# Second block's input projections as three rounded passes, their weights loaded and split by half blocks

## The chip, the cores and the metric

One core of one Trainium2 chip runs the whole program. The metric is device microseconds (us) of one execution; lower is better. PE is TensorE, DVE VectorE, ACT ScalarE, POOL GpSimd, and SP the engine whose queue issues nearly all DMAs.

## The reference, cut to what matters

Two blocks follow each other. The first (two layers of gated attention, pooling and an MLP) gives `x`, 256 tokens of 1024. The second takes `x` and a context of 256 tokens:

```python
hl = rms_norm(xl, norm1_gain[layer]) * (1.0 + sc1l) + sh1l        # 256 latent tokens
hc = rms_norm(xc, norm1_gain[layer]) * (1.0 + sc1c) + sh1c        # 256 context tokens
pl = hl @ w_in[layer]
pc = hc @ w_in[layer]
al, bl, cl = jnp.split(pl, [A_PROJ, A_PROJ + B_PROJ], axis=-1)
...
a_lat, a_ctx = hgrn2_mixer(...)              # columns a: aq, ff, fb, ai, ag
b_lat, b_ctx = rwkv7_mixer(...)              # columns b
c_lat, c_ctxo = neighbourhood_attention(...) # columns cq, ck, cv
xl = xl + g1l * (jnp.concatenate([a_lat, b_lat, c_lat], axis=-1) @ w_out[layer])
... xl = xl + g2l * hierarchical_moe(h2l)    # 32 experts
```

All is float32. `w_in_2` is 1024 x 3968; the change is about `hl @ w_in` and `hc @ w_in`.

## The kernel before

Five instruction streams are written by hand and meet at semaphores. The first block splits each float32 operand in two rounded halves (type fp32r): `high` is a rounded copy made on ACT, `low` is what is left, made on DVE. A product is then three passes, high*high, low*high and high*low, summed in PSUM (`split_rows`, and L1345 for `down`). Weights go by half blocks of 8 x 256 columns: one ACT copy (L1840, L1842), one DVE subtraction (L2268, L2271), which writes `low` over the raw weights in the ring `wring` (`w_low` is the same memory). The second block does its projections in plain float32 instead: `project` (L1398, L1405) multiplies the raw blocks in `wring` with `hT` (8 tiles of 128 channels x 512 tokens). A plain float32 matmul leaves two records in the trace, a rounded pass one.

The order of the second block is the list `MIXER_STEPS`, which PE, ACT and DVE all walk: the projections of a, cq; then `carry` and `diag`; then seven times (`level` n, one of ck0 to ck3, cv0 to cv2); `cross`, cv3, `hsum`, then b0 to b7 between `window`, `qsum`, `ksq`, `qnorm`, `rope`, `knorm`, `vtok`, `kunit`; then the chunked inverse of the b mixer (`group` steps, which end with the job GT 3). Each product is a job with one of eight PSUM banks; a bank is opened when the job that held it has been emptied (`EARLIER2`). ACT takes most projections out of PSUM (L2031, L2042, L2053); b jobs end on DVE (`shift`, L2544 and L2545). In each level DVE makes the factors of the next level (`level_f`, L2556 to L2567), then puts four masked products in place (L2733); POOL makes those of the other direction (L3062 to L3073).

The weights of the projections are nine blocks of up to 2 MB in two slots of `wring`, slots 0 and 1; a block is loaded when the last job of the block before it in its slot is done. Slots 2 and 3 hold work data by then. After GT 3 the two blocks of `w_out_2` are loaded, and behind them on the same queue the experts' weights, 96 blocks of 2 MB in twelve slots, each slot as it comes free.

At the very start PE spreads the gain row `norm1` over the partitions through PSUM (L1277), DVE multiplies it into `x` (L2326), and PE turns the result (L1199), before the first products (L1227).

Of the kernel before, what the change touches and what calls it, by code (L numbers as in the profile page):

```python
# [13 lines left out]
P = 128  # L14
# [179 lines left out]
for _name, _n in (("norm1_gain_2", 8), ("rwkv_mu_2", 9), ("rwkv_kk_scale_2", 2),  # L194
# [9 lines left out]
BLOCKS2 = [("w_in_2", c, n) for c, n in ((0, 512), (512, 512), (1024, 256), (2432, 512), (2944, 512), (3456, 512),  # L204
                                         (1280, 512), (1792, 512), (2304, 128))]
N_BASE_DMA, N_EARLY_DMA, N_MOD_DMA = 13, 3, 4
EXPERT_ORDER = (4, 2, 3, 5, 6, 7, 8, 0, 9, 1, 10, 11)
BLOCKS2 += [("w_out_2", 512 * j, 512) for j in range(2)]
SLOT2 = [0, 1, 0, 1, 0, 1, 0, 1, 0] + [0, 1]
TURN2 = [SLOT2[:n + 1].count(SLOT2[n]) for n in range(len(BLOCKS2))]  # L210
B_WOUT = 9


BEFORE2 = [("ff", 1), ("ai", 1), ("ag", 0), ("cq", 1), ("ck", 3), ("cv", 3), ("b", 2), ("GT", 3), ("GT", 3)]


PROJ_C = {("aq", 0): (0, (0, P), S), ("ff", 0): (0, (2 * P,), 2 * S), ("ff", 1): (0, (3 * P,), 2 * S),
          ("fb", 0): (1, (0,), 2 * S), ("fb", 1): (1, (P,), 2 * S),
          ("cq", 0): (3, (0, P), S), ("cq", 1): (3, (2 * P, 3 * P), S),
          ("b", 0): (6, (0, P), S), ("b", 1): (6, (2 * P,), 2 * S), ("b", 2): (6, (3 * P,), 2 * S),  # L220
          ("b", 3): (7, (0,), 2 * S), ("b", 4): (7, (P,), 2 * S), ("b", 5): (7, (2 * P,), 2 * S),
          ("b", 6): (7, (3 * P,), 2 * S), ("b", 7): (8, (0,), S)}
PROJ_C.update({("ck", j): (4, (j * P,), 2 * S) for j in range(4)})
PROJ_T = {("ai", j): (1, (2 * j, 2 * j + 1), 2 * P, 4 * P) for j in range(2)}
PROJ_T.update({("ag", 0): (2, (0, 1), 0, 2 * P)})
PROJ_T.update({("cv", j): (5, (j,), 0, 4 * P) for j in range(4)})
# [26 lines left out]
def mixer_steps():  # L253


    steps = [("proj", job) for job in (("aq", 0), ("ff", 0), ("ff", 1), ("fb", 0), ("fb", 1), ("ai", 0), ("ai", 1), ("ag", 0),
# [3 lines left out]
    for n in range(len(LEVELS)):  # L260
# [5 lines left out]
              ("rope", 3), ("proj", ("b", 7)), ("kunit", 1), ("bstart", 0)]  # L266
    i = 0
# [34 lines left out]
def second_plan():  # L302
    both = ("act", "dve")
    jobs = [("vec", 0, "dve")]
    jobs += [("xc", j, both[j % 2]) for j in range(4)] + [("xl", j, both[j % 2]) for j in range(4)]
# [50 lines left out]
for _name, _j, _e in JOBS2:  # L356
    _count[_e] += 1
    EMPTIED2[(_name, _j)] = (_e, _count[_e])


def second_banks():


    order = [job[:2] for job in JOBS2 if job[0] != "wout"]
# [91 lines left out]
def build(nc, d, out):  # L456

    ctx = ExitStack()
    with ctx:
# [7 lines left out]
        def rounded_views(*pieces):  # L467


            with ExitStack() as over:  # L470
                return [over.enter_context(nc.sbuf_tensor(name, shape, F32R if name[:3] != "gap" else F32))
                        for name, shape in pieces]
# [18 lines left out]
                                           ("at_low", [P, HEADS_PER_GROUP, S]))  # L491
        R = sb("R", [P, R_SIZE])
# [43 lines left out]
        ones_row = R[0:1, 0:P]  # L536
        by_rms = R[:, P:P + ST * P].rearrange("p (t s) -> p t s", t=ST)
# [19 lines left out]
        first_in, ones_set, gain_full = sem("first_in"), sem("ones_set"), sem("gain_full")  # L557
# [103 lines left out]
        gmoe = part(D)  # L661
        mod2 = part(2, KT)
        mulT = part(3, KT)
        turn_area = at[0]
        base = part(P + 64 + 18 * 64)
# [4 lines left out]
        gmix = part(D)  # L670
# [13 lines left out]
        kam = part(2)  # L684
        route_area = at[0]
# [17 lines left out]
        fF, fB, kF, kB = part(2, T2), part(2, T2), part(2, T2), part(2, T2)  # L703
        ai, ag = part(4, A_W), part(2, A_W)
        hg_mask = part(len(LEVELS) * 2 * P // 4).bitcast(mybir.dt.uint8).rearrange("p (m t) -> p m t", t=P)
        junk2 = R[:, a_area:a_area + D]
        hT = part(KT, T2)
# [6 lines left out]


# [160 lines left out]
        def wait_block2(eng, n):  # L876

            eng.wait_ge(loaded[SLOT2[n]], 16 * (NB1 // SLOTS + TURN2[n]))

# [9 lines left out]
        def expert_loads(sw_, pair, m):  # L889

            each = 16 * 2 * TURN_BLOCKS // SLOTS_X
            i = expert_slot(m)
            earlier_loads = NB1 // SLOTS + SLOT2.count(i) if i < SLOTS else 0
            return sw_ * (TURNS // 2 * each) + pair * each + 16 * (earlier_loads + m // SLOTS_X + 1)
# [17 lines left out]
        def shift_parts(j):  # L912

            if j == 0:
                return [(pB_r[:, 0, :], 0, S, 0), (pB_r[:, 1, :], S, S, 1)]
            if j < 5:
                return [((pB_k, pB_v)[(j - 1) // 2][:, (j - 1) % 2, :], 0, T2, 1 + j)]
            return [((pB_w, pB_a, pB_g)[j - 5], 0, (T2, T2, S)[j - 5], 1 + j)]

# [4 lines left out]
        def _(sp):  # L924
# [47 lines left out]
            def early_load(j):  # L972
# [48 lines left out]
                elif j == 10:  # L1021
# [6 lines left out]
                    sp.wait_ge(sumsq2, 2)  # L1028
                    for i in range(2):
                        sp.dma_start((gmix, gmoe)[i].rearrange("p (q n) -> p q n", q=2),  # L1030
                                     mod_at(2 + 3 * i, 0, [[0, P], [SLOTS_E * 512, 2], [1, 512]])).then_inc(mod_in, 16)
# [4 lines left out]
            for t in range(ST):  # L1036
                sp.dma_start(h[:, t, :], d["x"][0, t * P:(t + 1) * P, :]).then_inc(h_in[t], 16)
            for n, (l, name, j) in enumerate(BLOCKS1):
# [51 lines left out]
            def load2(n):  # L1090
                name, c, width = BLOCKS2[n]
                dst = wring[:, SLOT2[n], 0:KT * width].rearrange("p (k n) -> p k n", k=KT)
                sp.dma_start(dst, d[name][0].rearrange("(k p) n -> p k n", p=P)[:, :, c:c + width])\
                    .then_inc(loaded[SLOT2[n]], 16)

            for n in range(len(BLOCKS2)):

                if n < 2:
                    wait_free(NB1 - SLOTS + n)
                else:  # L1100
                    wait_full2(sp, BEFORE2[n - 2])
                load2(n)
                if n == 1:
# [3 lines left out]
                if n == 2:  # L1107
                    sp.wait_ge(rpb_out, 16)
                    for q in range(2):
                        for r in range(6):  # L1110
                            src = bass.AP(tensor=rpb_dram.tensor, offset=(1 - q + r) * P,
                                          ap=[[1, 64], [7 * P, C_HEADS], [1, 64]])
                            sp.dma_start(nhank[64 * q:64 * q + 64, :, r, :], src).then_inc(nhank_in, 16)

# [32 lines left out]
        def _(pe):  # L1147
# [7 lines left out]
            def bias_table():  # L1155
# [10 lines left out]
                mm.then_inc(cols_full, 1)  # L1166

# [15 lines left out]
            for l in range(DEPTH):  # L1183
# [182 lines left out]
            def mix_out(j, ks, last):  # L1366

                half, t = j // 2, j % 2
                if not last:
                    wait_block2(pe, B_WOUT + half)  # L1370
# [5 lines left out]
                for k in ks:  # L1376
                    mm = pe.matmul(b[:, :], mixT[:, k, t * P:(t + 1) * P], w2(B_WOUT + half)[:, k, :],
# [6 lines left out]
            def w2(n):  # L1384
                width = BLOCKS2[n][2]
                return wring[:, SLOT2[n], 0:KT * width].rearrange("p (k n) -> p k n", k=KT)

            def project(name, j):

                in_channels = (name, j) in PROJ_C  # L1390
                n = (PROJ_C if in_channels else PROJ_T)[(name, j)][0]
                wait_block2(pe, n)
                b = fill(name, j)
                if in_channels:
                    _, tiles, width = PROJ_C[(name, j)]
                    for i, c in enumerate(tiles):
                        for k in range(KT):
                            mm = pe.matmul(b[:, i * width:(i + 1) * width], w2(n)[:, k, c:c + P], hT[:, k, 0:width],  # L1398
# [1700 lines left out]
```

## Time and profile before

| | |
|---|---|
| median of 3 runs | 1932.03 us (1921.66 to 1933.64) |
| profiled execution | 1936.39 us, span 1934.6 us |
| PE, DVE, ACT, POOL busy | 89%, 45%, 31%, 6% of the span |
| moved by DMA | 419.44 MB, mean 217 GB/s |

The span is the time from the first to the last record of one profiled execution. Busy shares are means over stages with different limits; the rows below are therefore read by stretches.

### The profile page before, as it was taken

Reading aid. Unit: us, or ns where it says so; the run is one execution under the profiler, and the core shown is the slowest. Engines: PE = TensorE matmul, PEld = TensorE weight load, DVE = VectorE, ACT = ScalarE, POOL = GpSimd, SP = SyncE. Lnnn points to the kernel's source line nnn. Section 1 sums busy time; section 2 is a strip of 40 time slices with the busy share of each in tenths; the row PEclk is TensorE's granted clock in tenths of the full one; section 3 lists DMA queues with packets and bytes.
Section 4 is the critical chain, followed back from the end, with each engine's and each line's share of the span. In section 5 each row is a group of like instructions: output and inputs, shape, how many; then the busy total and the mean of one; then the engine's idle time right before and its main releaser. Section 6 shows DMA issues by size and latency. Waiting matters only on the chain.

```text
span 1934.6 us, 32462 instructions
## 1 busy us (share of the span) xinstructions
PE 1729.6 (89%) x14383; PEld 1316.1 (68%) x14383; DVE 865.5 (45%) x1203; ACT 594.0 (31%) x768; POOL 114.8 (6%) x103
## 2 busy tenths in 40 slices
PE   7999999999999999999999999789987867767676
PEld 6999998997799999899857564578854222212221
DVE  4445556664444555666432745886524111101111
ACT  4435445443434544455321011333313000000000
POOL 0500000000050000000012420000000000000000
PEclk9999999999999999999999999899998887777877
DMA  7552365745775236596525110000089999999997
GB/s 278 212 199 77 131 234 219 277 176 182 256 256 200 75 131 234 219 331 216 177 50 141 59 44 11 2 3 3 4 316 396 409 410 409 409 410 410 409 410 290
DMA packets 154833, 419.44 MB, mean 217 GB/s; under 512 B 14051, under 2 KB 20894, under 8 KB 151636
## 3 DMA queue, kind: packets, MB, share of 16 engines
q1 hardware_dynamic: 154274, 417.35, 58.2%
q8 instruction: 103, 1.69, 0.4%
q10 hardware_dynamic: 434, 0.22, 0.0%
q14 instruction: 22, 0.18, 0.0%
HBM read 415.66 MB, written 1.89 MB: 216 GB/s over the span
## 4 chain that ended last, share of the span: by engine, by line
PE 63%; DMA 20%; DVE 9%; ACT 5%; issue 2%; SPq 1%; ACTq 0%; DVEq 0%
PE bank L1227 30%; DMA R<-w_exp_up 9%; DMA R<-w_exp_down 9%; PE ps_s L1345 3%; PE bank L1398 3%; PE ps_s L1398 3%; PE ps_t L1345 3%; ACT w_high L1842 2%; PE bank L1423 2%; PE bank L1796 2%; PE ps_t L1405 1%; DVE w_low L2271 1%; DMA wring<-w_up 1%; SPq L1126 1%; PE ps_t L1398 1%
## 5 line engine op out<-in xcount | busy, mean ns | idle before, releaser
L2271 DVE TENSOR_TENSOR w_low<-wring,w_high 128x2048 fp32r<-128x2048 f32 (+1 forms) x127 | 285.2, 2245 | 312.9 <-ACT w_high L1842 312.5
L1842 ACT ACTIVATE w_high<-wring 128x2048 fp32r<-128x2048 f32 (+1 forms) x127 | 236.2, 1860 | 341.1 <-PE bank L1227 297.4
L1227 PE MATMUL bank<-x_high,w_high 128*128 128x256 f32 x1600 | 326.2, 285 | 9.7 <-DVEq L2317 7.4
L1227 PE MATMUL bank<-x_low,w_high 128*128 128x256 f32 x1600 | 321.6, 283 | 0.0
L1227 PE MATMUL bank<-x_high,w_low 128*128 128x256 f32 x1600 | 320.3, 282 | 0.0
L1227 PEld LDWEIGHTS bank<-x_high,w_high 128*128 128x128 f32 x1600 | 248.2, 191 | 16.8 <-DVEq L2317 8.5
L1227 PEld LDWEIGHTS bank<-x_high,w_low 128*128 128x128 f32 x1600 | 248.1, 190 | 0.0
L1227 PEld LDWEIGHTS bank<-x_low,w_high 128*128 128x128 f32 x1600 | 247.1, 190 | 0.0
L1796 PE MATMUL bank<-R 128*32 128x512 f32 x640 | 96.5, 736 | 48.1 <-DMA R<-w_exp_up 37.8
L1796 PEld LDWEIGHTS bank<-R 128*32 128x32 f32 x640 | 19.6, 124 | 118.7 <-DMA R<-w_exp_up 65.0
L2986 DVE TENSOR_TENSOR R<-bank,R 128x512 f32<-128x512 f32 x8 | 5.5, 694 | 210.3 <-PE bank L1796 210.3
L2268 DVE TENSOR_TENSOR w_low<-wring,w_high 128x2048 fp32r<-128x2048 f32 x22 | 50.4, 2292 | 60.3 <-ACT w_high L1840 60.3
L1796 PE MATMUL bank<-wring,R 128*32 128x512 f32 x384 | 53.2, 677 | 22.4 <-DMA wring<-w_exp_up 22.4
L1227 PE MATMUL bank<-w_high,x_high 128*128 128x256 f32 x320 | 64.7, 284 | 5.0 <-issue 3.2
L1811 PE MATMUL ps_s<-R 128*32 128x512 f32 x192 | 32.8, 760 | 38.2 <-DMA R<-w_exp_down 32.7
L2994 DVE TENSOR_TENSOR R<-ps_s,R 128x512 f32<-128x512 f32 x8 | 5.5, 692 | 136.0 <-PE ps_t L1811 136.0
L1227 PE MATMUL bank<-w_high,x_low 128*128 128x256 f32 x320 | 64.4, 283 | 0.0
L1227 PE MATMUL bank<-w_low,x_high 128*128 128x256 f32 x320 | 63.9, 281 | 0.0
L1840 ACT ACTIVATE w_high<-wring 128x2048 fp32r<-128x2048 f32 x22 | 42.1, 1916 | 70.9 <-PE ps_t L1345 58.0
L2193 ACT ACTIVATE R<-bank,R 128x128 f32<-128x128 f32 x32 | 12.1, 456 | 168.6 <-PE bank L1778 168.6
L3026 POOL TENSOR_TENSOR R<-R 128x542 f32<-128x542 f32 (+3 forms) x20 | 33.0, 1650 | 497.7 <-ACT R L1871 496.3
L1398 PE MATMUL bank<-R,wring 128*128 128x256 f32 (+1 forms) x192 | 54.9, 445 | 2.6 <-DMA wring<-w_in 1.5
(617 smaller groups left out, 2731.9 us busy)
## 6 DMA issues: line engine op xcount, KB each, us to landing
wring<-w_in SPq DMA_DIRECT2D x36, 2048.0 KB, 8.2
R<-w_exp_up SPq DMA_DIRECT2D x24, 2048.0 KB, 24.0
R<-w_exp_down SPq DMA_DIRECT2D x24, 2048.0 KB, 23.8
wring<-w_up SPq DMA_DIRECT2D x22, 2048.0 KB, 9.2
R<-w_exp_gate SPq DMA_DIRECT2D x16, 2048.0 KB, 23.4
wring<-w_exp_gate SPq DMA_DIRECT2D x16, 2048.0 KB, 23.7
wring<-w_ada SPq DMA_DIRECT2D x12, 2048.0 KB, 10.3
wring<-w_down SPq DMA_DIRECT2D x10, 2048.0 KB, 7.7
```

The lines of the kernel that those rows point to most:

```text
L1126: sp.dma_start(expert_block(m).rearrange("p (u k n) -> p u k n", u=QUAD, k=k), src[:, :, k * c:k * c + k, :]).then_inc(loaded[s], 16)
L1227: mm = pe.matmul(b[:, i * S:(i + 1) * S], left, right, start=k == 0 and m == 0 and i == 0, stop=k == last and m == 2, skip_group_check=True)
L1345: mm = pe.matmul(down_bank[j], left, ww[:, kk, half * 512:(half + 1) * 512], start=i == 0 and kk == 0 and m == 0, stop=i == N_DOWN - 1 and ...
L1398: mm = pe.matmul(b[:, i * width:(i + 1) * width], w2(n)[:, k, c:c + P], hT[:, k, 0:width], start=k == 0, stop=k == KT - 1)
L1423: mm = pe.matmul(b[q, 64 * o:64 * o + 64], lhs(q, c), rhs(q, c), start=start, stop=stop, skip_group_check=skip)
L1796: mm = pe.matmul(banks8[2 + which][q, :], xg[:, k, q], ww[:, u, k % 2, :], start=k == 0, stop=k == KT - 1)
L1811: mm = pe.matmul(banks8[5 + half][q, :], hidT[:, k, q], ww[:, u, half * 512:(half + 1) * 512], start=k == 0, stop=k == D_EXP // P - 1)
L1840: a.activation(down_high(l, job[1]), down_rows(l, job[1], wring), ACT.Copy).then_inc(w_high_ready, 1)
L1842: a.activation(high_of(l, job), half_block(l, job, wring), ACT.Copy).then_inc(w_high_ready, 1)
L2268: v.tensor_tensor(down_rows(l, job[1], w_low), down_rows(l, job[1], wring), down_high(l, job[1]).bitcast(F32), ALU.subtract).then_inc(w_lo ...
L2271: v.tensor_tensor(half_block(l, job, w_low), half_block(l, job, wring), high_of(l, job).bitcast(F32), ALU.subtract).then_inc(w_low_ready, 1)
L3026: chain(g_eng.tensor_tensor(dst[:, :, 0:m], src[:, :, 0:m], src[:, :, w:w + m], ALU.add))
```

## The change

1. The inputs of the projections are split: `hT_high` on ACT, `hT_low` on DVE, tile pairs at a time, the 256 latent tokens before the 256 of the context. All their PSUM banks now count as emptied when DVE's `low` is written.
2. `project` makes three rounded passes.
3. `w_in_2` comes as 16 half blocks (`IN2`) in four half slots, in the memory of slots 0 and 1. Half block n is loaded when the last job of n - 4 is done. Its `high` is written to one of five areas of the second block's store that are free by then (`HOME2`), its `low` over the raw weights. The two steps of each split stand in the ACT and DVE streams as the steps `split` of `MIXER_STEPS`, behind the job that `SPLIT_BEHIND` names; block 0 is split in the last layer's `down`, blocks 1 and 2 between the two halves of the inputs.
4. The job ag comes after aq; DVE's first part of `carry` becomes a step `carry_in` behind fb1.
5. Loads of `gmix` and `gmoe` move behind b7, those of `nhank` from behind block 2 to behind half block 12.
6. At the start the gain row is loaded to all partitions by one DMA of 512 KB on SP's queue, ahead of the first weights; PE's spreading products are gone.
7. PE issues products whose result nobody reads (`keep_clock`): 6 at the start, 6 before the first `products` step, 5 before the router's counts, 2 before the experts, each a plain float32 matmul of 128 x 128 by 512 columns.

```diff
+IN2 = [(0, 256), (1024, 256), (256, 256), (512, 256), (768, 256), (2432, 256), (2688, 256), (2944, 256), (3200, 256),
+       (3456, 256), (3712, 256), (1280, 256), (1536, 256), (1792, 256), (2048, 256), (2304, 128)]
...
+HOME2 = "EXGECGECGECEFEFE"
+TAKEN_FROM = {2: None, 3: ("aq", 0), 4: ("xc", 3), 5: ("ff", 1), 6: ("fb", 1), 7: ("ai", 1), 8: ("cq", 0), 9: ("cq", 1),
+              10: ("ck", 1), 11: ("cv", 1), 12: ("ho", 1), 13: ("b", 0), 14: ("b", 2), 15: ("b", 4)}
+SPLIT_BEHIND = {("aq", 0): 3, ("ag", 0): 4, ("ff", 1): 5, ("fb", 1): 6, ("ai", 1): 7, ("cq", 0): 8, ("ck", 0): 9, ("ck", 1): 10,
+                ("cv", 1): 11, ("b", 0): 13, ("b", 2): 14, ("b", 4): 15}
...
+            if g == ("fb", 1):
+                with_splits.append(("carry_in", 0))
+        if step == "hsum":
+            with_splits.append(("split", 12))
...
+            for n, (c, width) in enumerate(IN2):
+                if n in (0, 2):
+                    wait_free(NB1 - SLOTS + n // 2)
+                elif n > 3:
+                    wait_full2(sp, LAST_JOB[n - 4])
+                if n == 5:
+                    sp.wait_ge(high2_ready, 3)
+                sp.dma_start(raw2(n, wring), w_in2[:, :, c:c + width]).then_inc(sem_of_in2(n), 16)
...
             def project(name, j):
...
+                pe.wait_ge(low2_ready, n + 1)
                 b = fill(name, j)
...
+                for k in range(KT):
+                    if k % 2 == 0 and job in (("aq", 0), ("ff", 0)):
+                        wait_emptied2(pe, ("xl" if name == "aq" else "xc", k // 2))
+                    for m, (wx, xx) in enumerate(((ww[0], hT_high), (ww[0], hT_low), (ww[1], hT_high))):
+                        for i, c in enumerate(tiles):
+                            left, right = (wx[:, k, c:c + P], xx[:, k, 0:width]) if in_channels else \
+                                (xx[:, k, c * P:(c + 1) * P], wx[:, k, :])
+                            mm = pe.matmul(b[:, i * width:(i + 1) * width], left, right, start=k == 0 and m == 0 and i == 0,
+                                           stop=k == KT - 1 and m == 2, skip_group_check=True)
...
+            def high_in2(n):
+
+                a.wait_ge(sem_of_in2(n), loads_of_in2(n))
+                if n >= 3:
+                    wait_full2(a, TAKEN_FROM[n])
+                a.activation(high2(n), raw2(n, wring), ACT.Copy).then_inc(high2_ready, 1)
...
+                    ins.then_inc(hT_act, 1)
+                    a.wait_ge(hT_act, (first + j) // 2 + 1)
+                    rounded(j)
+                    a.wait_ge(hT_dve, (first + j) // 2 + 1)
+                    rounded(j + 1)
...
+            high_in2(1)
+            x2_evac("xl", 0, 0)
+            high_in2(2)
+            x2_evac("xc", 1, 4)
...
+            def low_in2(n):
+
+                v.wait_ge(high2_ready, n + 1)
+                v.tensor_tensor(raw2(n, w_low), raw2(n, wring), high2(n).bitcast(F32), ALU.subtract).then_inc(low2_ready, 1)
...
+                for j in range(4):
+                    v.wait_ge(hT_ready, first + j + 1)
+                    v.tensor_tensor(hT_low[:, 2 * j:2 * j + 2, part_of], hT[:, 2 * j:2 * j + 2, part_of],
+                                    hT_high[:, 2 * j:2 * j + 2, part_of].bitcast(F32), ALU.subtract).then_inc(dve_emptied2, 1)
...
+            x2_evac("xl", 0, 0)
+            low_in2(1)
+            low_in2(2)
+            x2_evac("xc", 1, 4)
...
                 if l == 0:
-                    pe.wait_ge(ones_set, 1)
-                    pe.wait_ge(gain_in, 16)
-                    for half in range(2):
-                        mm = pe.matmul(ps_t[:, half * 512:(half + 1) * 512], ones_row, grow[0:1, half * 512:(half + 1) * 512],
-                                       start=True, stop=True)
-                    mm.then_inc(gain_full, 1)
+                    pe.wait_ge(idle_set, 1)
+                    keep_clock(bank[3][:, :], idle_in[:, 0:P], idle_in, 6)
...
                 elif stage == "products":
+                    if g == 0:
+                        keep_clock(open_bank("tk", 0)[:, :], ident[:, :], h[:, 0, 0:512], 6)
                     pe.wait_ge(group_ready, g + 1)
...
+            b = fill("tot", 0)
+            keep_clock(b[:, :], ident[:, :], h[:, 1, 512:1024], 5)
             pe.wait_ge(moe_c_in, 32)
             pe.wait_ge(sel_ready, 1)
...
+            keep_clock(banks8[3], ident[:, :], h[:, 1, 512:1024], 2)
             pe.wait_ge(rt_done, 1)
```

## Rows read from the trace of the kernel before

**Rows 1.** The page's first part: busy us, share of the span, instructions.

```profile
PE 1729.6 (89%) x14383; PEld 1316.1 (68%) x14383; DVE 865.5 (45%) x1203; ACT 594.0 (31%) x768; POOL 114.8 (6%) x103
```

**Rows 2.** Chain of waits over the span, second block: start, us, what.

```profile
985.65 22.87 PE bank L1398 x64
...
1036.12 8.28 DMA wring<-w_in
...
1065.64 7.08 PE ps_s L1398 x16
...
1133.27 7.06 PE ps_t L1405 x16
...
1190.71 8.94 PE ps_s L1398 x16
...
1242.29 4.51 PE bank L1423 x96
1246.80 1.87 PE ps_s L1423 x64
```

**Rows 3.** Windows: us; PE, PEld, DVE, ACT, POOL busy; PEclk, DMA share, GB/s.

```profile
985.65:1058.60 72.95, 71.50 (x258) 50.01 (x259) 8.50 (x15) 9.91 (x16) 15.29 (x12) 0.97 0.41 94
1058.60:1133.30 74.70, 74.40 (x393) 44.22 (x391) 57.16 (x80) 6.31 (x11) 34.23 (x48) 1.00 0.17 57
1133.30:1226.80 93.50, 90.95 (x340) 49.26 (x341) 48.84 (x72) 17.17 (x26) 1.71 (x1) 0.96 0.09 28
985.60:990.00 4.40, 4.35 (x11) 3.54 (x12) 2.93 (x6) 0.00 (x0) 0.00 (x0) 0.54 0.01 4
1234.00:1242.30 8.30, 0.01 (x2) 0.01 (x2) 7.96 (x13) 6.86 (x15) 0.00 (x0) 0.58 0.00 0
1430.00:1455.00 25.00, 23.51 (x332) 16.89 (x329) 9.38 (x23) 4.10 (x7) 0.00 (x0) 1.00 0.78 295
...
1476.60:1500.00 23.40, 21.70 (x174) 10.79 (x178) 3.76 (x14) 5.36 (x9) 0.00 (x0) 0.90 1.03 409
```

**Rows 4.** Chain of waits, first block: rounded passes that wait for nothing.

```profile
146.44 5.71 PE bank L1227 x48
...
467.66 2.80 PE ps_s L1345 x12
```

**Rows 5.** Timeline of ACT: a weight split, then projections taken out of PSUM.

```profile
965.38 1.92 ACT L1840 ACTIVATE w_high<-wring 128x2048 fp32r<-128x2048 f32 x1 [3.68 <-PE ps_t L1345]
...
994.80 0.60 ACT L2031 ACTIVATE R<-bank 128x512 f32<-128x512 f32 x1 [10.08 <-PE bank L1398]
...
1058.59 0.60 ACT L2031 ACTIVATE R<-bank 128x512 f32<-128x512 f32 x1 [6.32 <-PE bank L1398]
```

**Rows 6.** Timeline of DVE: a weight split, one level, the last steps ahead of the groups.

```profile
967.33 2.29 DVE L2268 TENSOR_TENSOR w_low<-wring,w_high 128x2048 fp32r<-128x2048 f32 x1 [3.31 <-ACT w_high L1840]
...
1096.60 1.31 DVE L2567 TENSOR_TENSOR R<-R 128x128 f32<-128x128 f32 x1
...
1098.43 0.45 DVE L2567 TENSOR_TENSOR R<-R 128x128 f32<-128x128 f32 x1
1098.92 2.56 DVE L2733 COPY_PREDICATED wring<-R,bank 128x512 f32<-128x512 uint8 x4
...
1213.04 0.75 DVE L2544 SCALAR_TENSOR_TENSOR R<-ps_s,R 128x510 f32<-128x510 f32 x1 [5.44 <-PE ps_s L1623]
...
1229.16 0.69 DVE L2790 TENSOR_TENSOR wring<-wring 128x512 f32<-128x512 f32 x1
```

**Rows 7.** DMA issues by shape: count, KB each, median us to landing.

```profile
wring<-w_in SPq DMA_DIRECT2D x3, 1024.0 KB, 7.2
```

**Rows 8.** Chain of waits, the start.

```profile
6.37 3.79 PE ps_t L1277 x4
10.24 2.48 DVE R L2326 x4
...
21.34 22.88 PE bank L1227 x192
```

More of the change, by code:

```diff
@@ L207 @@
+N_BASE_DMA, N_EARLY_DMA, N_MOD_DMA = 13, 3, 2
 EXPERT_ORDER = (4, 2, 3, 5, 6, 7, 8, 0, 9, 1, 10, 11)
[L208 to L222, printed above, removed]
@@ L266, in mixer_steps @@
               ("rope", 3), ("proj", ("b", 7)), ("kunit", 1), ("bstart", 0)]
+    with_splits = []
+    for step, g in steps:
+        with_splits.append((step, g))
+        if step == "proj" and g in SPLIT_BEHIND:
+            with_splits.append(("split", SPLIT_BEHIND[g]))
+            if g == ("fb", 1):
+                with_splits.append(("carry_in", 0))
+        if step == "hsum":
+            with_splits.append(("split", 12))
+    steps = with_splits
     i = 0
@@ L302, in second_plan @@
 def second_plan():
-    both = ("act", "dve")
     jobs = [("vec", 0, "dve")]
-    jobs += [("xc", j, both[j % 2]) for j in range(4)] + [("xl", j, both[j % 2]) for j in range(4)]
+    jobs += [("xc", j, "dve") for j in range(4)] + [("xl", j, "dve") for j in range(4)]
     for step, g in MIXER_STEPS:
@@ L660, in build @@
         at[0] = 0
-        gmoe = part(D)
         mod2 = part(2, KT)
         mulT = part(3, KT)
+        at[0] += -at[0] % 16
+        e_area = at[0]
+        gmoe = part(D)
         turn_area = at[0]
+        gmix = part(D)
         base = part(P + 64 + 18 * 64)
@@ L1113, in _ @@
                             sp.dma_start(nhank[64 * q:64 * q + 64, :, r, :], src).then_inc(nhank_in, 16)
+            wait_full2(sp, ("b", 7))
+            for i in range(2):
+                sp.dma_start((gmix, gmoe)[i].rearrange("p (q n) -> p q n", q=2),
+                             mod_at(2 + 3 * i, 0, [[0, P], [SLOTS_E * 512, 2], [1, 512]])).then_inc(gmul_in, 16)
+            wait_full2(sp, ("GT", 3))
+            for half in range(2):
+                name, c, width = BLOCKS2[half]
+                sp.dma_start(w2(half), d[name][0].rearrange("(k p) n -> p k n", p=P)[:, :, c:c + width]).then_inc(loaded[half], 16)
             gates_d = [d[x].rearrange("a g e k n -> (a g e) k n") for x in ("w_exp_gate_2", "w_exp_up_2", "w_exp_down_2")]
@@ L1166, in bias_table, with keep_clock @@
                 mm.then_inc(cols_full, 1)
+            def keep_clock(b, left, right, n):
+                for _ in range(n):
+                    pe.matmul(b, left, right, start=True, stop=True)
             def modulate(l, i):
@@ L1995, in _ @@
                 for i in range(2, N_DOWN):
+                    if l == DEPTH - 1 and i == N_DOWN - 1:
+                        high_in2(0)
                     a.wait_ge(down_used, l * (N_DOWN - 1) + i - 1)
@@ L2016, in full_bank, with x2_evac, rounded @@
                 return bank2(*job)
-            def x2_evac(name, dst, w, mul, add):
+            def x2_evac(name, c, first):
+                part_of = slice(0, S) if c == 0 else slice(S, T2)
+                def rounded(j):
+                    a.activation(hT_high[:, 2 * j:2 * j + 2, part_of], hT[:, 2 * j:2 * j + 2, part_of], ACT.Copy).then_inc(hT_ready, 1)
                 for j in (0, 2):
@@ L2116, in _ @@
                     project(*g)
+                elif step == "split":
+                    high_in2(g)
                 elif step == "carry":
@@ L2693, in _ @@
                     shift(g[1])
-                elif step == "carry":
+                elif step == "split":
+                    low_in2(g)
+                elif step == "carry_in":
                     v.wait_ge(base_in, 16 * N_BASE_DMA)
```

153 lines of the change are left out of this document (78 added, 75 removed).

## The prediction

> **What bounds the kernel now.** I read the page first: PE is busy for 89% of the span [rows 1], which says where to look but not what is worth what. Then the chain of waits, which names what ended last at each time. From 985.65 us, where the second block's projections begin, it is PE nearly throughout [rows 2]: the windows give 71.5, 74.4 and 91.0 us of PE in stretches of 73.0, 74.7 and 93.5 us, with DVE at 8.5, 57.2 and 48.8 [rows 3]. So up to about 1213 us each microsecond taken off a projection comes off the path, as long as DVE keeps up; the middle stretch is the one to watch. From 1213.04 to the end of L2790 at 1229.85 the chain is DVE's, fed by the job b5 [rows 6]. The groups follow and end with GT 3 at some 1412 us, and this job releases w_out and the experts' weights on SP's queue. From there to the last expert DMA is the limit: 409 GB/s and a share of 1.03 in 1476.6 to 1500, with short gaps before it (0.78 in 1430 to 1455) [rows 3]. The expert stretch has a fixed length from GT 3 on: what is saved before GT 3 shifts the end one for one, and a faster PE after it saves next to nothing.
>
> **The passes.** The unit here is one projection of 128 output columns by 512 tokens (or as much work): 8 plain matmuls of 512 columns, 16 records, 7.08 us as channels, 7.06 as tokens [rows 2]. After the change it is 24 rounded passes of 512 columns or 48 of 256. Twelve of the first kind take 2.80 us [rows 4], so 24 take 5.60; 48 of the second take 5.71 [rows 4]. Both rows are in the same number format with their weight loads hidden, so I take them as they are. There are 25.5 units: a and cq 10, ck and cv 8, b0 7.5. By stretches:
>
> - *aq.* Now it starts at 985.65 and ACT takes it at 994.80 [rows 5], 9.15 us, because the granted clock is 0.54 in 985.6 to 990, near the lower of its two levels, 1.2 GHz, after a pause of PE [rows 3]; that stretch gives about 2.2 us of work less than 2.4 GHz would. Afterwards aq waits tile pair by tile pair. The turned latent inputs arrive at 982.4 as now; ACT makes two 0.5 us evacuations and two rounded copies of 0.6 us per pair of jobs, DVE the same share plus 0.69 us for each `low` (my estimate from the 512-element rows of the same kinds of instruction). The first pair is split at about 985.1, the last at 987.7. With the same 2.2 us lost, 5.71 becomes 7.9: done at 993.0, a gain of **1.8**. Bounds: warm at once 3.9; nothing before the last pair, 0 or 1 lost.
> - *ag, ff, fb, ai, cq.* Now 63.8 us from 994.80 to 1058.59 [rows 5]. This holds a wait of 1.4 us at 1044.4 for the load that was issued at 1036.12 [rows 2]. Afterwards 4 x 5.60 + 5 x 5.71 = 51.0: gain **12.8**. The context tiles are split by 997, ff0 asks for them at 998.7. The wait goes, since half block n is asked for only three blocks after its load is issued: at least 20 us here against 7.2 to landing [rows 7] plus 4.2 for the split.
> - *Levels and cv3.* 1065.64 to 1133.27 is 67.6 us [rows 2] and holds seven projections, 49.6; afterwards 4 x 5.60 + 3 x 5.71 = 39.5. With 1.35 on cv3 the gain is 11.4, if DVE keeps up. DVE now has 57.2 us of work in 74.7 [rows 3]; splits 9, 10 and 11 add 3 x 2.29 [rows 6], 64.0 us in a stretch of 63.3. It is then full. What saves PE is that it asks only for the first two products of `level_f`, a projection later. I walked it through: a level step of DVE is 7.44 us (1094.04 to 1101.48; its last 2.56 us are the masked copies [rows 6]), a PE period 8.35. Split 9 also makes DVE wait for ACT (ck0 done, 0.6 evacuation, 1.92 copy [rows 5]). After splits 9 and 10 DVE is late by about one split, and the fourth product of level 3 finds its bank not emptied for 1.4 us. I take 1.5 off: gain **9.9**.
> - *b0 to b5.* These six take 43.8 us in the chain, one of them 8.94 at a lowered clock behind products of only 8 rows [rows 2]. Afterwards 5.71 + 4 x 5.60 + 7.8 for the slow one, 35.9: gain 7.9. Split 12 stands behind `hsum`, where ACT has 3.9 us of squares first; block 12 is ready as b1 wants it, within 0.2 us. Splits 12 and 13 make DVE late for `hout` and the first window products, so the last window waits some 1 us for a bank. Gain **6.9**.
> - *After b5* the DVE chain of 16.8 us [rows 6] stays as it is; split 15 lies before it. b6 and b7 lie beside it, worth nothing. Second block together: 1.8 + 12.8 + 9.9 + 6.9 = **31.4**.
>
> **Splits of the weights.** 16 x 1.92 us of ACT and 16 x 2.29 us of DVE [rows 5, 6]. In the stretches of rows 3 ACT has 9.9, 6.3 and 17.2 us of work, so ACT is nowhere near full; DVE hides all but the levels, as said. Behind a waiting `high_in2` on ACT are the evacuations of the next job; the loads are long in. Block 0 is split in `down`, where DVE idles 3.31 us before each split [rows 6]: 0. Queue SP: 16 issues in place of 9, the twelve of nhank moved behind half block 12, with b0's load (13) due only when cv1 is done: 0. gmix and gmoe behind b7 are wanted 200 us later: 0.
>
> **The start.** PE's spreading goes (6.37 to 10.16) and the DVE products can begin when the gain row is in. Rows of 512 KB from h land 1.3 us after each other, so I estimate 7.6 instead of 10.24 [rows 8]. The first turn would be ready at 11.3. But six idle products stand before it. At the rate of rows 8 (0.95 us a record, two records each) they take 11.4 us and end at 17.7; at full rate 5.3. Six products are dense work like aq's, so I take aq's loss, 2.2 us [rows 3]: 7.5 us, an end near 13.5, since the load of the identity is no longer second on its queue and lands some 0.5 us sooner, and then turns at full rate. DVE is then last: L1227 at 19.6 instead of 21.34, gain **1.7**. Bounds: 2.5 gained, 3.3 lost. The weights come 1.3 us later for the 512 KB, covered by 20 us.
>
> **The fills.** PE is idle in 1234 to 1242.3 at 0.58 of the clock, and the first 96 products then take 4.51 us where 64 take 1.87 later [rows 2, 3]; at that rate 2.8. Six fills of 5.3 us (7.5 with the 2.2 lost) end before 1242.3: gain **1.7**, bounds 2.5 gained and 2.4 lost if they run slow all along. The other seven are behind GT 3 under the DMA: 0, and 0 if slow, since at 1476 about three expert blocks of 5 us each are still to land before PE's first slot is wanted.
>
> **Sum.** 31.4 + 1.7 + 1.7 = 34.8. The profiled execution gives 1936.4 - 34.8 = 1901.6. It lies 4.4 above the median of the runs; from the median, 1932.0 - 34.8 = **1897**.
>
> **Rivals.** *A, DVE and POOL hold the levels.* L2567 takes 1.31 us with POOL at work and 0.45 after [rows 6]: the two slow each other. If each of splits 9, 10 and 11 keeps POOL's factors waiting for its 2.29 us and this passes to PE, 6.9 us go, and some 4 more where DVE is late for the windows: 1908. The Trainium skill, page "SBUF — State Buffer", section "Summary: rules for kernel authors", says a DVE instruction with two SBUF inputs and a GpSimd one that reads SBUF exclude each other for a whole instruction; the 1.31 agrees, and by it each split can hold POOL up for 2.29. Against A: POOL has 34.2 us of work in 74.7 [rows 3], and its factors are wanted one projection, 5.6 us, after they are begun. *B, slower: the splits are not hidden.* If blocks 1 to 15 were each split when PE already waits, 15 x (1.92 + 2.29) = 63 us come on the path: 1897 + 63 = 1960. It turns the sign when 2.3 us of each are exposed. Against it: all but split 12 stand two or more jobs before their use. *C, it gives more:* runs like the lowest of before (1921.7) on a shift of 36 give 1886. *D, the fills cost in both places* (3.3 and 2.4 lost in place of 1.7 and 1.7 gained): 9 us less, 1906.
>
> **How the numbers follow.** Forecast 0.60, A 0.16, D 0.09, C 0.08, B 0.03, and 0.04 for a gain under 1% by some stall that I don't see. The range must hold the forecast, A, C and D: 1885 to 1911. A change of under 1%, 19 us, can't be told from none here; the threshold is 1912.7, which A and D stay below: of these cases 0.93 lie below it, and I leave 0.03 of A's for a dearer stall: faster 0.90, same 0.07, slower 0.03.
>
> **What would show it.** Right: no L1398 or L1405 records of two per matmul; 24 passes in 5.6 us; no DMA wait ahead of cq; cq1 taken out at about 1042 (start shifts included), the chain at GT 3 near 1377; the first 96 group products in 2.8 us. A shows as PE waiting before `level` steps for POOL or DVE; B as PE waiting for DVE's `low` with ACT ahead of it; D as L1227 after 22 us. Wrong altogether if the rounded passes run slower with these operands than in the first block, or if the experts' stretch from GT 3 to the end, 522 us, changes.

## The result, and the profile after

The changed kernel takes **1904.3 us** (median of 4 runs, 1897.3 to 1906.0) against 1929.7 of before beside it (1921.7 to 1933.6): ratio 0.987, 95% interval 0.984 to 0.989. On two more chips it came to 0.985 [0.983, 0.986] and 0.983 [0.981, 0.986], 29.8 and 29.7 us less by the medians. So the change gives 25 to 30 us; 34.8 were forecast. The profiled execution took 1903.4, 33.0 less than that of before.

The page of after, its first part and the granted clock in 40 slices:

```profile
PE 1712.9 (90%) x14777; PEld 1347.8 (71%) x14777; DVE 907.9 (48%) x1227; ACT 627.0 (33%) x792; POOL 125.6 (7%) x103
...
PEclk9999999999999999999999999789999977767777
```

PE's share of the span hardly moves [rows 1], so this part says nothing of where 33 us went. In the clock's line a 7 and an 8 stand in slices 26 and 27 (1188.4 to 1283.5 us), where the groups begin. The chain of waits says more, piece by piece against rows 2 and 8: the start, the second block's first projection, the first level's projection, cv3, b4, and a piece of the groups.

```profile
5.29 7.88 PE bank L1222 x12
...
19.10 24.42 PE bank L1283 x192
...
981.55 18.68 PE bank L1451 x120
...
1046.88 5.78 PE ps_s L1451 x24
...
1107.67 5.91 PE ps_t L1451 x48
...
1159.59 7.82 PE ps_s L1451 x24
...
1183.13 3.36 DVE wring L2880
...
1258.51 2.85 PE bank L1469 x64
```

No DMA stands between 981.55 and cq: the load of 8.28 us at 1036.12 [rows 2] is gone from the chain. The last line is a product of 64 records that takes 1.87 us at the high clock [rows 2]. The same stretches in windows (columns as in rows 3): aq's beginning, all to the carry's products, the levels, the gates, the first expert loads, the end.

```profile
981.50:986.00 4.50, 4.45 (x27) 4.49 (x28) 4.23 (x5) 4.44 (x7) 0.00 (x0) 0.67 0.01 4
981.50:1045.00 63.50, 63.15 (x435) 58.47 (x436) 37.03 (x39) 29.48 (x36) 22.01 (x16) 0.97 0.39 117
1046.80:1107.60 60.80, 60.22 (x449) 53.09 (x448) 56.55 (x72) 10.02 (x11) 37.81 (x42) 1.00 0.31 79
1192.70:1203.40 10.70, 10.70 (x17) 4.34 (x17) 8.90 (x10) 5.77 (x8) 0.00 (x0) 0.50 0.29 58
...
1448.00:1471.00 23.00, 20.55 (x182) 8.95 (x186) 4.41 (x18) 5.66 (x9) 0.00 (x0) 1.00 1.02 409
1891.90:1901.50 9.60, 5.62 (x24) 1.85 (x24) 4.24 (x7) 0.00 (x0) 0.00 (x0) 0.99 0.30 109
```

PE is as full as before in the first two stretches, and they are shorter. DVE is busy for 56.6 of 60.8 us in the levels. The fourth line is the gates (products L1500 and L1502, 16 records, behind b7): they run at a granted clock of 0.50, which is 1.2 GHz, and over the 7.2 us of the gates before the clock was 0.76. The fifth is the expert loads' 409 GB/s, the same as before [rows 3].

The timeline of ACT answers to rows 5 (aq and cq1 taken out of PSUM), that of PE shows what became of the gates, of the fills behind them and of the first group products:

```profile
991.55 0.58 ACT L2096 ACTIVATE R<-bank 128x512 f32<-128x512 f32 x1
...
1039.83 0.60 ACT L2096 ACTIVATE R<-bank 128x512 f32<-128x512 f32 x1 [3.31 <-PE bank L1451]
```

```profile
1192.70 2.04 PE L1500 MATMUL bank<-R 64*128 64x512 f32 x2 [3.87 <-issue]
...
1203.37 7.87 PE L1222 MATMUL bank<-h,ident 128*128 128x512 f32 x12
1211.18 3.02 PE L1469 MATMUL bank<-ident,wring 64*64 64x64 f32 x96
```

Before, the gates ran from 1226.80 to 1233.97 behind a pause of PE of 2.56 us. Now the pause is 3.87 and they take 10.7. The fills then take 7.9 and end only as the products begin: DVE's input for these was ready at 1210.91, so the slow fills held them back by some 0.2 us.

From these points come the stretches of every kernel (us, the start of one piece less the start of another; L2880, L2789 in before, is the reciprocal behind b5; "last load" is where the last w_exp_down lands):

| kernel | first block's products | second block's | to L2880 | to group products | to w_out | to last load | to end |
|---|---|---|---|---|---|---|---|
| before | 21.3 | 985.7 | 231.0 | 25.6 | 170.2 | 508.2 | 14.0 |
| before, second profile | 21.3 | 982.3 | 230.7 | 25.6 | 170.5 | 508.2 | 12.5 |
| after | 19.1 | 981.6 | 201.6 | 28.0 | 172.5 | 508.2 | 9.6 |
| c0_after | 18.9 | 980.2 | 203.0 | 26.9 | 173.7 | 507.3 | 13.0 |
| c1_after | 19.3 | 982.3 | 201.6 | 26.8 | 172.9 | 508.6 | 9.7 |
| e1_no_fills | 19.1 | 979.2 | 201.6 | 26.8 | 171.2 | 506.7 | 11.1 |
| e2_gates_fill | 18.6 | 979.0 | 203.2 | 25.0 | 172.1 | 508.1 | 11.0 |
| e3_split10_later | 19.2 | 980.2 | 202.4 | 26.2 | 170.0 | 507.6 | 9.7 |
| e4_no_low_levels | 19.0 | 981.8 | 201.2 | 26.0 | 169.9 | 507.5 | 9.6 |
| e5_plain | 18.9 | 980.0 | 231.9 | 26.8 | 170.8 | 508.6 | 11.2 |
| e6_pauses_filled | 18.0 | 980.9 | 201.0 | 25.1 | 169.6 | 507.6 | 9.6 |
| e6b_pauses_filled | 18.7 | 979.8 | 201.9 | 25.0 | 170.2 | 507.2 | 11.1 |
| e7_start_as_before | 21.5 | 984.9 | 202.8 | 26.0 | 169.9 | 507.5 | 9.6 |
| e9_end_fills | 19.2 | 980.1 | 202.4 | 25.0 | 170.1 | 508.1 | 9.7 |

Between before and after: 29.4 us gained in the projections, 2.2 at the start and 1.9 more until 981.55; 2.4 lost ahead of the group products and 2.3 in the groups; 4.4 gained at the end, which is no part of the change, as c0_after shows with 13.0 for the same kernel.

### The profile page after: what moved, and what is told of

Read it like the earlier page. It is cut to its first block, busy times and chain, and to the rows that moved or that the text cites. A ratio compares the mean times of both kernels' runs of the same rounds, so it can differ in the third digit from the quotient of the medians.

```text
span 1901.5 us, 33316 instructions
## 1 busy us (share of the span) xinstructions
PE 1712.9 (90%) x14777; PEld 1347.8 (71%) x14777; DVE 907.9 (48%) x1227; ACT 627.0 (33%) x792; POOL 125.6 (7%) x103
## 4 chain that ended last, share of the span: by engine, by line
PE 62%; DMA 19%; DVE 10%; ACT 6%; issue 2%; DVEq 0%; ACTq 0%
PE bank L1283 30%; DMA R<-w_exp_up 9%; DMA R<-w_exp_down 9%; PE bank L1451 3%; PE ps_s L1397 3%; PE ps_t L1397 3%; ACT w_high L1889 2%; PE ps_s L1451 2%; PE bank L1469 2%; PE bank L1843 2%; DVE w_low L2344 2%; PE ps_t L1451 2%; DMA wring<-w_up 1%; PE ps_t L1469 1%; PE ps_s L1469 1%
## 5 line engine op out<-in xcount | busy, mean ns | idle before, releaser
L1843 PE MATMUL bank<-R 128*32 128x512 f32 x640 | 102.7, 778 | 51.3 <-DMA R<-w_exp_up 40.2
L1858 PE MATMUL ps_s<-R 128*32 128x512 f32 x192 | 35.6, 821 | 38.2 <-DMA R<-w_exp_down 34.8
L2274 ACT ACTIVATE R<-ps_s 128x512 f32<-128x512 f32 x8 | 4.8, 600 | 152.5 <-PE ps_s L1848 152.5
```

The costliest lines, as they stand in the source:

```text
L1843: mm = pe.matmul(banks8[2 + which][q, :], xg[:, k, q], ww[:, u, k % 2, :], start=k == 0, stop=k == KT - 1)
L1858: mm = pe.matmul(banks8[5 + half][q, :], hidT[:, k, q], ww[:, u, half * 512:(half + 1) * 512], start=k == 0, stop=k == D_EXP // P - 1)
```

## The experiments

The changed kernel ran on the same chip as some of them: c0_after with e1 to e3, c1_after with e6b, e7 and e9. b0_before, e4, e5 and e6 ran on a third chip without it; before has medians of 1929.0, 1932.8 and 1930.9 us on the three, so medians of different chips can differ by 4 us without cause in the code.

**c0_after, c1_after: the changed kernel again.** No edit.

> The changed kernel once more, on the chip of the next three. If the profiled execution was typical, the group fills' stretch and the two pauses behind it (near 1231 and 1258 us) again show a granted clock near 0.6, the gates at 1192 a clock near 0.5, and the median lies at 1903 +- 3. If the low clock there was the luck of one execution, those stretches show 0.8 to 1.0 and the profiled time is 5 to 8 us lower, near 1896.

> The changed kernel once more, as the measure for the next three on the same chip: 25 to 31 us under the kernel before. Its stretches repeat within 1.5 us where PE's clock is high (second block's first projection to the first reciprocal of keys 201.6 to 203.0, first product of w_out to the last expert load 507 to 508.5); reciprocal to w_out and the end behind the last load vary with the granted clock (198.5 to 201, and 9.6 to 14).

Medians 1899.2 and 1903.0, single runs from 1896.5 to 1905.9. The low clock behind b7 is no luck of one execution: 1188.8 to 1300 shows a granted clock of 0.85, 0.86 and 0.86 in the three profiles. The end is luck; its difference is PE's clock after the last load, 0.99 over the end in after and 0.76 in c0_after. These are timeline lines of after (upper two) and of c0_after (lower two):

```profile
1891.91 1.06 PE L1858 MATMUL ps_s<-R 128*32 128x512 f32 x8 [1.43 <-DMA R<-w_exp_down]
1892.80 1.04 PE L1858 MATMUL ps_t<-R 128*32 128x512 f32 x8
```

```profile
1891.05 1.94 PE L1858 MATMUL ps_s<-R 128*32 128x512 f32 x8 [3.15 <-DMA R<-w_exp_down]
1892.76 1.81 PE L1858 MATMUL ps_t<-R 128*32 128x512 f32 x8
```

**b0_before: the kernel before again.** No edit.

> The kernel before, profiled once more. If its first profiled execution was a slow one of its own range (1936.4 against a median of 1929), this one's groups or its end differ in their granted clock and the time is 1924 to 1930; the stretch from the second block's first projection to b5, 219 us, is the same within 1 us in both.

1931.9 us. 230.7 against 231.0 in the second block; the first block was 3.4 us shorter and the end 1.5. A profiled pair can thus differ by some 5 us from the medians without any cause in the code. The second block's projections begin at 982.3 here, as early as in c1_after.

**e5_plain: the passes alone.**

```diff
-  for m, (wx, xx) in enumerate(((ww[0], hT_high), (ww[0], hT_low), (ww[1], hT_high))):
+  for m, (wx, xx) in ((0, (high2(n).bitcast(F32), hT_high.bitcast(F32))),):
```

> Every second-block projection is one plain product of the rounded weights and rounded inputs in place of the three rounded passes (the low parts are still made, but not multiplied, so the low parts are left out of the result); splits, order, loads and fills stay. Theory 1, that the passes are the whole gain: 24 passes of 5.6 to 5.8 us become 16 records of 7.1, 14 us more for the ten units to cq, some 10 for the levels and cv3, 7 to 8 for b0 to b5, together 31 to 33 more than the changed kernel: 1931, that is before again. Rival, that order, smaller loads and fills bring part of it: less than 27 us more than the changed kernel, under 1926.

1925.8 us (10 runs, 1920.0 to 1931.3), ratio 0.997 [0.996, 0.998]. Its chain, first level and cv3:

```profile
1059.16 7.06 PE ps_s L1451 x16
...
1126.86 7.10 PE ps_t L1451 x32
```

67.7 us, as before (67.6). The stretch to L2880 is 231.9: the passes are worth 30.3 us of it against after (28.9 against c0_after), and order, smaller loads and splits together cost 0.9 to 1.2 against the two profiles of before. So in the second block theory 1 holds. The rival's number came about in the whole time: 24 us over the mean of the changed kernel, 1901.6, and 5 under before. Of the 5, 2.4 are the start; the profiled execution was the slowest of the ten (1931.3), so where the rest lies is not shown.

This run says one thing more, of the stage behind the projections. With plain products PE's pause ahead of the gates is as short as before, and still the gates begin at the low clock and take 8.6 us:

```profile
1222.03 2.04 PE L1500 MATMUL bank<-R 64*128 64x512 f32 x2 [2.55 <-issue]
```

**e4_no_low_levels: what DVE's splits cost the levels.** The half blocks are those of cv0 to cv3 and b0. The kernel leaves out the low parts of these weights and multiplies the high parts once more in their place; PE's work stays as it was.

```diff
+  kk = 1 if n in (9, 10, 11) else KT
-  v.tensor_tensor(raw2(n, w_low), raw2(n, wring), ...)
+  v.tensor_tensor(raw2(n, w_low)[:, 0:kk, :], raw2(n, wring)[:, 0:kk, :], ...)
-  ww = (high2(n), raw2(n, w_low))
+  ww = (high2(n), high2(n) if n in (9, 10, 11) else raw2(n, w_low))
```

> The low parts of half blocks 9, 10 and 11 are made for one of eight slices only, and their third pass multiplies the high part again (so the low part of these weights is left out of ck0 to ck3's neighbours cv0 to cv3 and of b0's inputs in block 11); PE's and ACT's work is unchanged, DVE loses 3 x 2 us. Theory 1, that DVE's splits cost the levels only the 1 to 2 us of one late bank: cv3 starts 1 to 2 us earlier against aq's start, 1898. Rival A, that each split holds POOL and the levels for its whole length: cv3 starts 5 to 6 us earlier, 1893.

```profile
1047.12 5.78 PE ps_s L1451 x24
...
1105.92 5.85 PE ps_t L1451 x48
```

58.8 us against 60.8: the splits cost **2.0**, not 5 to 6. Rival A falls. The time, 1895.4 us (ratio 0.981 [0.980, 0.983]), lies lower than 2.0 explains; the rest is in the groups, 195.9 us from L2880 to w_out against 199.6 to 200.6, on code that was not touched.

**e3_split10_later.**

```diff
-  ("ck", 1): 10,
+  ("ck", 3): 10,
```

> The split of half block 10 stands behind ck3 instead of behind ck1. Theory 1, that two splits in two neighbouring level steps (2.29 and 3.07 us of DVE) make the fourth product of level 3 wait for its bank: PE's wait of some 4 us before ck3 goes and less than 1 us of it comes back later, cv3 is done 3 us earlier and the kernel takes 1900. Rival, that DVE is full over the whole of the levels: the wait only moves behind the place of the split, and the time is that of the changed kernel within 1 us.

1898.5 us, 0.7 less than c0_after. First level to cv3 is 60.1 in place of 60.8. The changed kernel has two waits here, 0.8 us ahead of ck2 and 1.1 ahead of ck3. The second is gone, the first has stayed, and a new one of 0.5 has opened ahead of cv1. So more than half of what was to be gained went as the rival said; DVE has 57 us of work in 60. But its five runs lie within 1.2 us (1897.6 to 1898.8) where c0_after's spread over 8.7, and from L2880 to w_out it took 196.1.

**e1_no_fills: all idle products out.**

```diff
-  keep_clock(bank[3][:, :], idle_in[:, 0:P], idle_in, 6)
+  keep_clock(bank[3][:, :], idle_in[:, 0:P], idle_in, 0)
-  keep_clock(open_bank("tk", 0)[:, :], ident[:, :], h[:, 0, 0:512], 6)
-  keep_clock(b[:, :], ident[:, :], h[:, 1, 512:1024], 5)
-  keep_clock(banks8[3], ident[:, :], h[:, 1, 512:1024], 2)
```

> All four groups of idle products are taken out (6 at the start, 6 ahead of the group products, 5 + 2 behind GT 3), the direct load of the gain row stays. Theory 1, that the fills pay where PE waits anyway: the first 96 group products go back from 3.0 to about 4.5 us (1.5 lost), the start loses 0 to 2, the tail nothing: 1.5 to 3.5 us more than the changed kernel, about 1906. Rival, that the gain at the start comes from the load of the gain row alone and the group's chain is DVE's: within 1 us of the changed kernel.

1901.0 us, 1.7 more than c0_after and well inside the intervals. Its chain at the start:

```profile
1.65 6.35 DMA R<-norm
8.09 2.50 DVE R L2400 x4
...
19.12 22.88 PE bank L1283 x192
```

Without fills the first block starts at the same 19.1. The start's gain is the early gain row: DVE begins at 8.09 in place of 10.24 [rows 8]. The fills ahead of the group products save 1 to 2 us there (the first 96 take 5.24 us without them, 3.02, 3.02 and 4.18 in the three profiles with) and nothing that shows in the time.

**e7_start_as_before.** The gain comes as one row over ScalarE's queue and is spread by PE, without idle products:

```diff
-  gain_row(0, "norm1")
-  keep_clock(bank[3][:, :], idle_in[:, 0:P], idle_in, 6)
+  mm = pe.matmul(ps_t[:, half * 512:(half + 1) * 512], idle_in[0:1, 0:P], grow[0:1, ...], ...)
-  v.tensor_tensor(xn[:, t, c], h[:, t, c], grow[:, c], ALU.mult)
+  v.tensor_tensor(xn[:, t, c], h[:, t, c], ps_t[:, c], ALU.mult)
```

> The start is that of the kernel before (gain as one row over ScalarE's queue, spread by PE, no idle products), all else as changed. Theory 1, that the early load of the gain row gives the start and the idle products nothing: the first block's first projection at 21.3 instead of 19.0, all that follows 2.2 us later, the kernel 2 us slower than the changed one. Rival, that the start has no part in it (the first block waits for its loads later on and swallows it): the second block's first projection stands where it stands in the changed kernel, 979 to 981.8, and so does the end.

The first block starts at 21.45, and the second block's projections at 984.9, where eleven profiles with the early row, with the fills or without, stand at 979.0 to 982.3. The two profiles of before, also with the late row, have 985.7 and 982.3, so the start's gain probably carries through, but the two groups touch. The median, 1903.6, is only 0.5 above c1_after; in its profile this kernel took 195.9 us from L2880 to w_out, 3.7 less. So the 2 us are shown at the first products and not in the time.

**e2_gates_fill: the clock of the gates.**

```diff
   elif step == "bstart":
+      keep_clock(open_bank("wz", 0)[:, :], ident[:, :], h[:, 0, 0:512], 4)
       pe.wait_ge(qk_turned, 1)
```

> Four more idle products right behind b7, ahead of PE's wait for the turned keys and the tanh. Theory 1, that the gates run at the low clock because PE pauses 3.9 us before them (2.6 before the change): the 16 records of the gates take 7.1 us instead of 10.8, the group products start 2 to 3.6 us earlier behind them, and the kernel takes 1900. Rival, that DVE's chain between gates and products sets their start anyway: the gates get faster and the products start where they did, 1903.

PE's timeline, the first gate and the first group products:

```profile
1191.78 1.09 PE L1500 MATMUL bank<-R 64*128 64x512 f32 x2 [0.43 <-issue]
...
1207.26 4.56 PE L1469 MATMUL bank<-ident,wring 64*64 64x64 f32 x96 [4.64 <-DVE wring L2729]
```

The gates are warm (at 2.4 GHz) and take 5.5 us, and from L2880 to the products it takes 25.0 in place of 26.9 us: the cold gates (at 1.2 GHz) did delay the chain through ACT and DVE. But now the six fills behind them end 4.6 us early and the products start cold again (4.56 us against 3.02). 1900.8 us against 1899.2, nothing gained. Theory 1 was right on the products' start, the rival on the time.

**e6_pauses_filled, e6b_pauses_filled:** e3's and e2's edits, and ahead of two waits of the groups

```diff
+  if (n, g) in ((1, 0), (3, 0)):
+      keep_clock(open_bank("XU", 8 * g + n)[:, :], ident[:, :], h[:, 0, 0:512], 3)
   wait_emptied2(pe, ("T1", 8 * g + n))
```

> The later split of half block 10, the four idle products ahead of the gates, and three more ahead of the waits of XMX1 and XMX3 of group 0, where PE paused 3 us and then ran at the low clock. Theory 1, that the low clock behind these pauses costs the groups 3 to 5 us in some executions: the granted clock stays over 0.95 from 1188 to 1300, the stretch from b7's end to the first product of w_out is 4 us shorter than in the changed kernel's profiled execution (191 in place of 195), and the runs lie closer, 1896. Rival, that DVE and ACT set the groups' pace: the clock is high and the stretch is as long as before, 1899.

> The same kernel as the one with its pauses filled, now beside the changed kernel on one chip. Theory 1, that 0.7 us in the levels, 1.9 ahead of the group products and 2 to 4 in the groups are real: 3 to 5 us less than the changed kernel, with the interval off zero. Rival, that its lower time was the chip's or a lucky clock: within 1.5 us of the changed kernel.

Windows of 1188.8 to 1300 us, of after and of e6_pauses_filled:

```profile
1188.80:1300.00 111.20, 99.54 (x1870) 77.83 (x1871) 88.53 (x164) 43.74 (x86) 0.00 (x0) 0.85 0.05 12
```

```profile
1188.80:1300.00 111.20, 101.57 (x2133) 81.64 (x2133) 89.50 (x167) 44.55 (x90) 0.00 (x0) 0.97 0.05 12
```

The clock rises from 0.85 to 0.97 (0.95 in e6b), and from L2880 to w_out it takes 194.7 and 195.2 us in place of 199.6 to 200.6. Medians 1895.8 and **1896.5**, the latter 6.6 less than c1_after on its chip; the ten runs lie at 1892.2 to 1898.8 (mean 1895.9), fourteen of the changed kernel at 1896.5 to 1906.0 (mean 1901.6), with a standard error of 1.2 on the difference of 5.7, over several chips; on the one chip that e6b shares with the changed kernel the means differ by 5.5, with 1.9. This version beats both kernels. What it does not show is that the filled pauses give the whole of it: e3, with the moved split and no new fill, already has 196.1 in that stretch and a mean of 1898.3. Beside e3 the fills are worth 1.0 to 1.4 us of the stretch and 2.4 of the mean, and the two ran on different chips.

**e9_end_fills.** e6's kernel, and in the expert turns

```diff
+  if odd and k >= 2:
+      keep_clock(banks8[3], ident[:, :], xs[:, 1, 0:512], 2)
   pe.wait_ge(loaded[expert_slot(m)], expert_loads(sw_, pair, m))
```

> The kernel with its pauses filled, and two idle products ahead of each of the last two down products of every second expert turn, where PE waits 1.4 to 3.2 us for a load. Theory 1, that the end behind the last load is 9.6 us at the high clock and up to 14 at the low one: it is 9.6 in every execution, 0 to 4 us less, 2 on the mean. Rival, that at the low clock two fills take 3.8 us where 2 are free, and so delay the release of the slots and the loads behind them: last load up to 4 us later, and the kernel slower by 1 to 3 us than the one with its pauses filled.

1896.7 us, as e6b. The profile has an end of 9.7 us, but the last load came 0.9 us later after w_out than in e6b. One profile each can't tell a gain at the end that is given back in the loads from none; this stays open.

## Why the prediction was right or wrong

The median lies in the range, and the mechanism of the large term was right. Two steps missed, and their sum, some 8 us less 0.5 for the start, lies within the 5 to 9 us between forecast and medians. One of the signs named failed by them: GT 3, after which w_out's first product starts, was to end near 1377, and that product starts at 1383.6.

- *aq to cq, 1.8 + 12.8.* From PE's start to cq1's take-out 72.9 us became 58.3, a gain of 14.7 (14.6 foreseen). The clock at aq's start was again low, 0.67. aq itself took PE 7.4 us, from 981.55 to 988.99 (7.9 foreseen). ACT took it out only at 991.55: ACT had waited 2.8 us for DVE, whose context evacuation stands behind two weight splits. That cost nothing, as PE was in ag.
- *Levels and cv3, 9.9: mis-sized, 8.0 measured* (6.8 + 1.2 on cv3). I took 2.80 and 5.71 from projections that follow each other. Here each follows another kind of product and takes 5.78 or 5.90, some 0.19 more; the 7.08 which I subtracted had this share in it, since a following one takes 6.88. That is 1.5 us. The other 0.5 is the stall: 2.0 by e4, 1.5 foreseen. The wait that was named, ahead of ck3, is 1.1 of it, and one ahead of ck2 0.8. Here is DVE's timeline around them:

```profile
1055.12 2.29 DVE L2350 TENSOR_TENSOR w_low<-wring,in_e 128x2048 fp32r<-128x2048 f32 x1
...
1065.18 3.07 DVE L2350 TENSOR_TENSOR w_low<-wring,in_c 128x2048 fp32r<-128x2048 f32 x1
1068.17 1.58 DVE L2644 TENSOR_TENSOR wring<-R,wring 128x512 f32<-128x512 f32 x1
```

  and POOL's beside it:

```profile
1055.55 3.01 POOL L3155 TENSOR_TENSOR wring<-R,wring 128x512 f32<-128x512 f32 x1 [3.25 <-PE bank L1485]
...
1064.80 1.30 POOL L3155 TENSOR_TENSOR wring<-R,wring 128x512 f32<-128x512 f32 x1 [2.27 <-PE ps_t L1485]
1066.18 3.02 POOL L3156 TENSOR_TENSOR wring<-R 128x512 f32<-128x512 f32 x1
...
1107.82 1.10 POOL L3156 TENSOR_TENSOR wring<-R 128x512 f32<-128x512 f32 x1 [0.78 <-PE ps_s L1485]
```

  POOL's factor takes 3.0 us beside a split and 1.1 in the last line, where no split runs. In e4, whose splits are short, the same two take 1.75 and 1.42, so a split costs POOL 1.3 to 1.6 us. The second split takes 3.07 in place of 2.29: it starts while POOL's L3155 runs to 1066.10, 0.8 us later. By the Trainium skill, page "SBUF — State Buffer", section "Summary: rules for kernel authors", of a DVE instruction with two SBUF inputs and a GpSimd one that reads SBUF the second to issue is held up until the first has finished. The trace agrees, with 3.01 and 3.07 us. But together the splits cost the levels only 2.0 us by e4, so rival A's 6.9 us did not come.
- *b0 to b5, 6.9.* Measured: 83.4 us from cv3's start to L2880 became 75.5, 7.9 less 1.2 of cv3's. Right. That b4 took 7.82 (7.8) is partly luck: its clock differs between kernels, and it took 7.4 in c1_after and 8.4 in e3.
- *Splits and loads elsewhere at 0.* Right: e5 has them all and its second block is 0.9 to 1.2 us longer than before. Rival B is out.
- *The start, 1.7.* 2.2 measured. The six idle products took 7.9 us (7.5 foreseen) and are neither gain nor loss; the gain row alone carries it.
- *"After b5 the DVE chain stays as it is" and "The fills ... gain 1.7": failed.* The chain of before does not stay on DVE until 1229.85, as I read it. It leaves DVE at 1224.51 and runs through PE's gates and ACT:

```profile
1224.51 2.29 issue
1226.80 1.11 PE bank L1456 x2
1227.95 0.03 issue
1227.98 1.28 ACT L2088
```

  So the gates' clock counts, and I had given them no term. From L2880 to the group products the changed kernel takes 26.8 to 28.0 us against 25.6, which loses 1.2 to 2.4; then the groups lose 2 to 3.5. Together that is 3.5 to 4.8 us lost where 1.7 was to be gained. That slow gates delay the products is shown by e2 (1.9 us). By removing the fills e1 shows that as placed they are worth nothing measurable; rival D's 5.7 us are out too. What made the gates and groups slow is not shown. The nearest cause is PE's pause: its end is set by DVE's and ACT's work behind b5, PE is now faster ahead of it, and so the pause grows from 2.56 to 3.87 us. But the length of the pause alone does not order the kernels:

| kernels | pause of PE | the gates take | L2880 to group products | L2880 to w_out | granted clock, 111.2 us from the gates on |
|---|---|---|---|---|---|
| before, second profile | 2.56 | 7.2 | 25.6 | 195.8, 196.1 | 0.91 |
| e5 | 2.55 | 8.6 | 26.8 | 197.6 | 0.93 |
| e4, e7 | 3.87 | 8.3 | 26.0 | 195.9 | 0.93 |
| e3 | 3.87 | 8.6 | 26.2 | 196.1 | 0.93 |
| e1 | 3.87 | 9.7 | 26.8 | 198.0 | 0.89 |
| c0_after, c1_after | 3.87 | 9.8, 9.7 | 26.9, 26.8 | 200.6, 199.6 | 0.87 |
| after | 3.87 | 10.7 | 28.0 | 200.5 | 0.85 |

  With the pause of before, e5's gates begin cold and its products come as late as c1_after's; with the long pause, e3, e4 and e7 take no longer to w_out than before did.
- *The expert stretch.* The loads' part is 508.2 us in before and after alike, and 506.7 to 508.6 in all profiles. The end behind them is 14.0 and 12.5 in the two profiles of before and 9.6, 13.0 and 9.7 in three of the changed kernel, longer where PE's clock is low; my fixed 522 was made of one value of it. That is why the profiled pair shows 33 us and the medians 25 to 30.
- *In the medians:* 34.8 - 1.9 (levels) + 0.5 (start) - 6 (groups) = 27, where 25.4, 29.8 and 29.7 were measured.

**What stays open:** why the groups take 199.6 to 200.6 us in three profiles of the changed kernel and 195.9 to 196.1 in e3, e4 and e7, whose code there is the same and only begins at another time (e5, also with this code, has 197.6). Their clock between 1188.8 and 1300 is 0.92 against 0.85 and 0.86. Open too is how much of e6's gain is the fills and how much the other moment at which its groups begin: no run has the fills with the split left in its place. The Trainium skill, page "TensorE: Matmul & The Clock Gate", section "Part 1: The HAM clock gate (the "warmup" mystery)", says that the chip judges PE's activity in a window that runs freely; a pause would then count or not by where it falls. The rows of e3, e4, e5 and e7 agree with it, and no run here set out to show it.

## What to carry to other kernels

Shortening PE's work ahead of a wait lengthens PE's pause at that wait: 2.55 us with plain products, 3.87 with rounded passes. Look at what stands behind it. Where that is PE work on a chain through ACT and DVE, its clock is on the path and wants a term of its own in the forecast. Idle products right ahead of such work kept its clock high here (the gates took 5.5 us against 9.8), and those that ended 4.6 us early did not. The fills in other places showed no gain. But the same code, fills unchanged, also ran 4 us faster when it began at another time, so a kernel that differs by a few us in such a stage needs more than one profile before its cause is named. And take the price of a new instruction and of the old one from rows in the same surroundings, both following their own kind or both following another.

## What the runs showed of the hardware that was not expected

- The same group code ran at a granted clock of 0.85 to 0.86 in three profiles of the changed kernel and of 0.92 in one profile each of e3, e4 and e7, over 111 us. From L2880 to w_out the first took 3.5 to 4.7 us longer.
- The end behind the last load takes 9.6 us in after with a granted clock of 0.99 over it (1.06 us for 8 records of L1858) and 13.0 in c0_after with 0.76 (1.94), so it changes between executions of one kernel.
- A projection that follows another kind of product takes some 0.19 us longer, rounded or plain: 5.78 against 5.60, 7.06 against 6.87.
